# Four weight slots at four other places modulo 512 bytes

## The chip, the cores and the metric

The kernel runs on one core of one Trainium2 chip. The metric is the device time of one execution in microseconds (us), the median over runs.

## The reference

One decoder layer on 256 tokens (`S`) of width 2048 (`D`), all in float32. Token mixing has two branches that read one projection: dilated sliding-window attention with 16 heads, and latent attention with 16 heads and a rotary key. Both are projected to width 2048, gated, summed and projected once more. Channel mixing then looks up experts (PEER): 16,384 single-neuron experts, of which 8 heads choose 16 each per token.

```python
proj = h @ w_in[l]
qa, ka, va, cq, ckv, kr, gate_pre = jnp.split(proj, IN_SPLITS, axis=-1)
...
y_a = y_a @ a_w_out[l]
...
y_b = y_b @ mla_w_out[l]
mix = (g_a * y_a + g_b * y_b) @ w_out[l]
h = layer_norm(ALPHA * h + mix, ln1_g[l], ln1_b[l])
y_p = peer(h, peer_w_query[l], peer_sub_keys_1[l], peer_sub_keys_2[l],
           peer_expert_down[l], peer_expert_up[l])
h = layer_norm(ALPHA * h + y_p, ln2_g[l], ln2_b[l])
...
def chunk(args):          # in peer(): xt tokens, et chosen experts, gt their gates
    xt, et, gt = args
    u = expert_down[et]
    h = jax.nn.gelu(jnp.einsum('cd,ced->ce', xt, u), approximate=False)
    vv = expert_up[et]
    return jnp.einsum('ce,ced->cd', gt * h, vv)
```

## The kernel before

All weights stand in one array, `stream`, in the order in which they are used: 425 tiles of 128 x 2048 float32, each in two halves of 128 x 1024 (4096 bytes per partition). A half goes through a pipeline of four slots, `slot = 2 * (tile % 2) + half`:

- SyncE loads the half into `raw[:, slot, :]`;
- ScalarE copies it to `w_hi[:, slot, :]`, rounded to the type fp32r (L355);
- VectorE writes the rest, `raw - w_hi`, to `w_lo[:, slot, :]` (L611);
- TensorE multiplies with `w_hi` and `w_lo` and then counts the half as used (`half_used`), which frees the slot.

Activations are split in the same way (`a_hi`, `a_lo`; `b_hi`, `b_lo`; `c_hi`, `c_lo`; `m_hi`, `m_lo`). Each product is then three matmuls: high by high, high by low, low by high. The experts aren't gathered: all 128 x 128 of them are computed, and a table `g_dram` of gates, zero where an expert isn't chosen, weighs them.

There are two shapes of product. Up to the down projections (`T_DN`), `three()` (L1011) loads a block of 128 x 128 weights and streams 256 columns of activations; a half is 8 blocks by 3, 24 matmuls. In a block, the operands alternate: `w_hi` with `a_hi`, `w_hi` with `a_lo`, `w_lo` with `a_hi`. In the last stage (`T_UP`, up projections), `up()` (L1208) exchanges the roles: it loads 128 x 128 of `m_hi` or `m_lo` and streams 512 columns of a slot; a half is 24 matmuls too. Weight blocks are 512 bytes apart, blocks of activations 1024 bytes, blocks streamed in the last stage 2048 bytes. So all matmuls of a slot have the same start modulo 512 bytes.

The place of a tensor follows from the order of the `sb(...)` calls, since each goes behind the last. `raw` starts at byte 16,512 of the partition, `w_hi` at 32,896 and `w_lo` at 49,280; each slot of them is 128 modulo 512. Behind them stand `small` (320 bytes), `stat` and `carrier` (64 each), which bring `a_hi`, `a_lo`, `res` and `cst` to 64 modulo 512. `gap_b` (384 bytes) does so for all that follows: `b_hi`, `b_lo`, `c_hi`, `c_lo`, `gate_a`, `head`, `m_hi`, `m_lo`. Nothing uses the gap.

The order on every engine is written out by hand with semaphores. Between the projections, TensorE has short work for attention (transposes L1058, scores L1052, products with `v`), sums by a matmul with `ones` (L1102, L1162; plain float32), and the scores of the keys (L1177).

Of the kernel before, what the change touches and what calls it, by code (L numbers as in the profile page):

```python
# [75 lines left out]
C_ID = C_ROPE + T  # L76
C_ONE = C_ID + P
C_IOTA = C_ONE + P
C_SLOPE = C_IOTA + P
C_TOKEN = C_SLOPE + HEADS  # L80
N_CONST = C_TOKEN + 16

# [46 lines left out]
def build(nc, stream, x_t, const_in, small_in, keys_t, ln2, y_out, a_dram, g_dram):  # L129
    ctx = ExitStack()  # L130

    def sb(name, shape, dt=F32, stack=ctx):
        return stack.enter_context(nc.sbuf_tensor(name, shape, dt))
# [3 lines left out]


    raw = sb("raw", [P, 4, HALF])
    w_hi = sb("w_hi", [P, 4, HALF], F32R)  # L140
    w_lo = sb("w_lo", [P, 4, HALF], F32R)
    small = sb("small", [P, N_SMALL])
    stat = sb("stat", [P, 16])
    carrier = sb("carrier", [P, 16])
    a_hi = sb("a_hi", [P, KD, T], F32R)
    a_lo = sb("a_lo", [P, KD, T], F32R)
    res = sb("res", [P, KD, T])
    cst = sb("cst", [P, N_CONST])
    sb("gap_b", [P, 96])

    mix_mem = ExitStack()
    b_hi = sb("b_hi", [P, KD, T], F32R, mix_mem)
# [99 lines left out]

    ident = col(C_ID, P)
    ones = col(C_ONE, P)
    iota = col(C_IOTA, P)
    block = ctx.enter_context(nc.Block())


# [86 lines left out]
    def _(act):  # L345
# [4 lines left out]
        def hi(t, halves=(0, 1)):  # L350

            for hf in halves:
                act.wait_ge(raw_in[t.slot(hf)], t.pair * 16 + 16)
                act.wait_ge(half_used, t.half(hf) + 1)
                act.activation(w_hi[:, t.slot(hf), :], raw[:, t.slot(hf), :], ACT.Copy).then_inc(hi_ready, 1)  # L355

        def done(t):
            act.wait_ge(half_used, t.half(1) + 1 + HALVES_FREE)
# [240 lines left out]
    def _(dve):  # L599
# [6 lines left out]
        def lo(t, halves=(0, 1)):  # L606

            for hf in halves:
                s = t.slot(hf)
                dve.wait_ge(hi_ready, t.half(hf) + 1)  # L610
                dve.tensor_tensor(w_lo[:, s, :], raw[:, s, :], w_hi[:, s, :].bitcast(F32), ALU.subtract).then_inc(lo_ready, 1)  # L611

        def done(t):
            dve.wait_ge(half_used, t.half(1) + 1 + HALVES_FREE)
# [386 lines left out]
    def _(pe):  # L1001
# [4 lines left out]

        def three(out, w_slot, c0, cn, act_h, act_l, first, last):

            wh, wl = w_hi[:, w_slot, c0:c0 + cn], w_lo[:, w_slot, c0:c0 + cn]
            for q, (w, a) in enumerate(((wh, act_h), (wh, act_l), (wl, act_h))):  # L1010
                ins = pe.matmul(out, w, a, start=first and q == 0, stop=last and q == 2)  # L1011
            return ins
# [186 lines left out]
        def up(t, n, b):  # L1199
            pe.wait_ge(mlo_ready, n + 1)  # L1200
            for hf in range(2):
                half_ready(t, hf)
                for tt in range(TT):
                    s = slice(P * tt, P * tt + P)
                    for m, w in ((m_hi, w_hi), (m_hi, w_lo), (m_lo, w_hi)):
                        for c in range(2):
                            o = D * tt + HALF * hf + 512 * c
                            ins = pe.matmul(ps[:, o:o + 512], m[:, b % 2, s], w[:, t.slot(hf), 512 * c:512 * c + 512],  # L1208
                                            start=False, stop=False, skip_group_check=True)
                ins.then_inc(half_used, 1)  # L1210

        def up_bank(t, b, tt, c):

            s = slice(P * tt, P * tt + P)
            o = D * tt + 512 * c
            w = slice(512 * (c % 2), 512 * (c % 2) + 512)
            pe.matmul(ps[:, o:o + 512], m_hi[:, b % 2, s], w_hi[:, t.slot(c // 2), w], start=False, stop=False, skip_group_check=True)
            pe.matmul(ps[:, o:o + 512], m_hi[:, b % 2, s], w_lo[:, t.slot(c // 2), w], start=False, stop=False, skip_group_check=True)
            return pe.matmul(ps[:, o:o + 512], m_lo[:, b % 2, s], w_hi[:, t.slot(c // 2), w], start=False, stop=False,
                             skip_group_check=True)  # L1220

        with pe.Fori(0, NKEYS // 8 - 1) as i:
# [20 lines left out]
def _constants():  # L1243

    c = np.zeros((P, N_CONST), np.float32)
    for b, (qt, kt) in enumerate(((0, 0), (1, 0), (1, 1))):
        q = np.arange(P)[:, None] + P * qt
        k = np.arange(P)[None, :] + P * kt
        d = q - k
        count = np.zeros((P, P), np.float32)  # L1250
        for window, dilation in PATTERNS:
            count += (d >= 0) & (d <= window) & (d % dilation == 0)
        s = slice(P * b, P * b + P)
        c[:, C_D:][:, s] = -d
        c[:, C_NA:][:, s] = np.where(count > 0, 0.0, NEG)
        c[:, C_NB:][:, s] = np.where(d >= 0, 0.0, NEG)
        c[:, C_C:][:, s] = count
    half = ROPE // 2
    inv_freq = np.float32(10000.0) ** (-np.arange(half, dtype=np.float32) / np.float32(half))
    ang = (np.arange(T, dtype=np.float32)[:, None] * inv_freq[None, :]).T  # L1260
    cos, sin = np.cos(ang), np.sin(ang)
    c[:, C_ROPE:C_ROPE + T] = np.concatenate([cos, cos, -sin, sin])
    c[:, C_ID:C_ID + P] = np.eye(P)
    c[:, C_ONE:C_ONE + P] = 1.0
    c[:, C_IOTA:C_IOTA + P] = np.arange(P)
    c[:, C_TOKEN:C_TOKEN + TT] = np.arange(P)[:, None] + P * np.arange(TT)[None, :]
    c[:, C_SLOPE:C_SLOPE + HEADS] = 2.0 ** (-8.0 * np.arange(1, HEADS + 1) / HEADS)
    return c
# [56 lines left out]
```

## Time and profile before

| | |
|---|---|
| median of three runs | 2482.05 us (2477.62 to 2502.12) |
| profiled execution: time, span | 2486.35 us, 2484.7 us |
| mean granted TensorE clock | 0.992 |
| TensorE matmul busy | 2450.2 us, 17,964 matmuls |
| VectorE, ScalarE, GpSimd busy | 1463.2, 1160.5, 549.1 us |
| HBM | 209 GB/s over the span |

Busy time is the union of an engine's instructions. A matmul's record covers its whole way through the array, so those of neighbours overlap; the interval from start to start is what one costs in a dense row. "PEld" is TensorE's weight load, which runs beside the matmul ahead of its own.

### The profile page before, as it was taken

The numbers are of one execution on the slowest core, as the hardware profiler recorded it, in microseconds if no ns is written. First come the engines' busy times: TensorE is split into PE (matmuls) and PEld (weight loads), VectorE is DVE, ScalarE is ACT, GpSimd is POOL, SyncE is SP. The second block draws the span as 40 slices with busy tenths as digits, with TensorE's granted clock in tenths as the row PEclk, the third lists the DMA queues.
The fourth block names the chain that finished last, engine by engine and source line by source line (L and its number), as shares of the span: only waits on it lengthen the run. The fifth ranks groups of instructions, "written<-read, shape, count | busy, mean of one in ns | idle before, by whom it ended". The sixth has DMA issues, their size and how long they took to land.

```text
span 2484.7 us, 49759 instructions
## 1 busy us (share of the span) xinstructions
PE 2450.2 (99%) x17964; PEld 2310.8 (93%) x17964; DVE 1463.2 (59%) x2391; ACT 1160.5 (47%) x1626; POOL 549.1 (22%) x379
## 2 busy tenths in 40 slices
PE   8999999999999998999999999999999999999997
PEld 8999999999999997999999999999888888888886
DVE  5555554546666655378888744444555555555556
ACT  4444444544444434455555544444444444444444
POOL 0000000000000003048888888810000000000000
PEclk9999999999999997999999999999999999999999
DMA  7667666554445653567788888876667666776664
GB/s 265 224 223 225 215 220 200 186 174 152 160 147 183 199 190 123 184 181 209 205 218 216 221 215 216 220 245 221 222 244 243 238 233 235 242 242 242 241 229 145
DMA packets 179840, 521.12 MB, mean 210 GB/s; under 512 B 52768, under 2 KB 52768, under 8 KB 179536
## 3 DMA queue, kind: packets, MB, share of 16 engines
q1 hardware_dynamic: 124128, 449.89, 54.2%
q0 software_dynamic: 51056, 53.89, 9.9%
q10 hardware_dynamic: 4608, 16.78, 1.7%
q8 instruction: 21, 0.34, 0.1%
q14 instruction: 27, 0.22, 0.0%
HBM read 484.70 MB, written 35.78 MB: 209 GB/s over the span
## 4 chain that ended last, share of the span: by engine, by line
PE 97%; DVE 2%; issue 1%; ACT 0%; DMA 0%; DVEq 0%; ACTq 0%
PE ps L1011 65%; PE ps L1208 28%; PE ps L1050 1%; PE ps L1065 1%; PE ps L1058 0%; PE ps L1052 0%; PE ps L1162 0%; PE ps L1177 0%; PE ps L1066 0%; PE ps L1045 0%; DVE a_lo L802 0%; DVE u_s L964 0%; DVE w_lo L611 0%; DVE u_s L974 0%; DVE y_s L951 0%
## 5 line engine op out<-in xcount | busy, mean ns | idle before, releaser
L611 DVE TENSOR_TENSOR w_lo<-raw,w_hi 128x1024 fp32r<-128x1024 f32 x850 | 1015.3, 1223 | 774.8 <-ACT w_hi L355 771.0
L1011 PE MATMUL ps<-a_hi,w_hi 128*128 128x256 f32 x3984 | 1121.0, 281 | 14.6 <-DVE w_lo L611 9.8
L1011 PE MATMUL ps<-a_lo,w_hi 128*128 128x256 f32 x3984 | 1110.0, 279 | 0.0
L1011 PE MATMUL ps<-a_hi,w_lo 128*128 128x256 f32 x3984 | 1109.9, 279 | 0.0
L355 ACT ACTIVATE w_hi<-raw 128x1024 fp32r<-128x1024 f32 x850 | 866.8, 1054 | 255.5 <-PE ps L1208 179.4
L1011 PEld LDWEIGHTS ps<-a_hi,w_hi 128*128 128x128 f32 x3984 | 752.9, 189 | 19.6 <-issue 15.3
L1011 PEld LDWEIGHTS ps<-a_lo,w_hi 128*128 128x128 f32 x3984 | 755.8, 190 | 0.5
L1011 PEld LDWEIGHTS ps<-a_hi,w_lo 128*128 128x128 f32 x3984 | 754.1, 189 | 0.0
L326 POOL DMA_INDIRECT g_dram<-gate_v,where x256 | 462.1, 1805 | 195.2 <-DVE gate_v L882 117.5
L1208 PE MATMUL ps<-w_lo,m_hi 128*128 128x512 f32 x1008 | 314.3, 393 | 0.0
L1208 PE MATMUL ps<-w_hi,m_hi 128*128 128x512 f32 x1008 | 312.7, 391 | 0.0
L1208 PE MATMUL ps<-w_hi,m_lo 128*128 128x512 f32 x1008 | 311.5, 390 | 0.0
L1208 PEld LDWEIGHTS ps<-w_hi,m_lo 128*128 128x128 f32 x1008 | 189.3, 188 | 43.1
L1208 PEld LDWEIGHTS ps<-w_lo,m_hi 128*128 128x128 f32 x1008 | 189.6, 188 | 40.9
L1208 PEld LDWEIGHTS ps<-w_hi,m_hi 128*128 128x128 f32 x1008 | 189.5, 188 | 39.9
L541 ACT ACTIVATE act<-ps 128x256 f32<-128x256 f32 x128 | 49.1, 384 | 323.6 <-PE ps L1011 322.4
L316 POOL DMA_DIRECT2D a_in<-a_dram x32 | 17.0, 532 | 751.7 <-DVE m_f L918 749.6
L535 ACT ACTIVATE m_hi<-m_f 128x256 fp32r<-128x256 f32 x128 | 53.4, 417 | 208.8 <-DVE m_f L918 208.8
L1011 PE MATMUL ps<-b_hi,w_hi 128*128 128x256 f32 x512 | 142.9, 279 | 0.0
L1011 PE MATMUL ps<-b_lo,w_hi 128*128 128x256 f32 x512 | 141.6, 277 | 0.0
L1011 PE MATMUL ps<-b_hi,w_lo 128*128 128x256 f32 x512 | 141.6, 276 | 0.0
L308 POOL TENSOR_SCALAR res<-res,small 128x256 f32<-128x256 f32 x16 | 18.0, 1139 | 503.1 <-DVE a_lo L802 503.1
(172 smaller groups left out, 1710.9 us busy)
## 6 DMA issues: line engine op xcount, KB each, us to landing
raw<-stream SPq DMA_DIRECT2D x850, 512.0 KB, 4.2
g_dram<-blank POOLq DMA_DIRECT2D x32, 512.0 KB, 6.2
a_dram<-act ACTq DMA_DIRECT2D x32, 512.0 KB, 3.6
a_in<-a_dram POOLq DMA_DIRECT2D x32, 512.0 KB, 4.9
g_in<-g_dram POOLq DMA_DIRECT2D x32, 512.0 KB, 6.2
g_dram<-gate_v,where POOLq DMA_INDIRECT x256
res<-x_t SPq DMA_DIRECT2D x4, 512.0 KB, 6.9
ln_s<-ln POOLq DMA_DIRECT2D x1, 2048.0 KB, 11.6
```

The source lines that it names most:

```text
L308: ins = pool.tensor_scalar(res[:, k, :], res[:, k, :], small[:, S_B1 + k:S_B1 + k + 1], None, ALU.add)
L316: pool.dma_start(a_in[:, b], a_dram[i * 2 + b]).then_inc(ag_in[b], 16)
L326: pool.indirect_dma_start(out=g_cell, out_offset=bass.IndirectOffsetOnAxis(ap=where[:, tt, k:k + 1], axis=0), in_=gate_v[:, tt, k:k + 1], ...
L355: act.activation(w_hi[:, t.slot(hf), :], raw[:, t.slot(hf), :], ACT.Copy).then_inc(hi_ready, 1)
L535: act.activation(m_hi[:, par, :], m_f[:, par, :], ACT.Copy).then_inc(mhi_ready, 1)
L541: act.activation(act4[:, b // 4, b % 4, :], acc[t.par][:, 0:T], ACT.Gelu).then_inc(acc_free[t.par], 1)
L611: dve.tensor_tensor(w_lo[:, s, :], raw[:, s, :], w_hi[:, s, :].bitcast(F32), ALU.subtract).then_inc(lo_ready, 1)
L1011: ins = pe.matmul(out, w, a, start=first and q == 0, stop=last and q == 2)
L1050: ins = pe.matmul(ps_s[:, o:o + k1], q_s[:, q0:q0 + P], k_s[:, 0:k1], start=True, stop=not rope)
L1065: pe.matmul(ps_o[:, 0:T], v_s[:, 0, :], p_t[:, 0:T], start=True, stop=False, skip_group_check=True)
L1208: ins = pe.matmul(ps[:, o:o + 512], m[:, b % 2, s], w[:, t.slot(hf), 512 * c:512 * c + 512], start=False, stop=False, skip_group_check=True)
```

## The change

`w_hi` and `w_lo` become four tensors each, one for each slot, and unused gaps and the small tensors `stat` and `carrier` stand between them, so that each slot has a start of its own modulo 512 bytes, the same for its high and its low part. To make room, `small` moves behind `cst` and takes the place of `gap_b` with it (320 bytes), and the constant `iota` shrinks from 128 to 16 columns, of which 16 were read.

| slot | start before, modulo 512 | start after (`w_hi`, `w_lo`) | after, modulo 512 |
|---|---|---|---|
| 0 | 128 | 32,928 and 53,920 | 160 |
| 1 | 128 | 37,120 and 58,112 | 256 |
| 2 | 128 | 41,280 and 62,272 | 320 |
| 3 | 128 | 45,504 and 49,600 | 448 |
| activations | 64 | `a_hi` 66,624, `b_hi` 124,480 | 64 |

`raw` stays where it was, and so does everything from `b_hi` on. `a_hi`, `a_lo`, `res` and `cst` move by 512 bytes or a few more and remain at 64 modulo 512. Each engine has the same instructions in the same order as before.

```diff
-C_SLOPE = C_IOTA + P
+C_SLOPE = C_IOTA + TOPK
...
     raw = sb("raw", [P, 4, HALF])
-    w_hi = sb("w_hi", [P, 4, HALF], F32R)
-    w_lo = sb("w_lo", [P, 4, HALF], F32R)
-    small = sb("small", [P, N_SMALL])
+    sb("gap0", [P, 8])
+    w_hi0 = sb("w_hi0", [P, HALF], F32R)
+    sb("gap1", [P, 24])
+    w_hi1 = sb("w_hi1", [P, HALF], F32R)
     stat = sb("stat", [P, 16])
+    w_hi2 = sb("w_hi2", [P, HALF], F32R)
+    sb("gap3", [P, 32])
+    w_hi3 = sb("w_hi3", [P, HALF], F32R)
+    w_lo3 = sb("w_lo3", [P, HALF], F32R)
     carrier = sb("carrier", [P, 16])
+    sb("gap4", [P, 40])
+    w_lo0 = sb("w_lo0", [P, HALF], F32R)
+    sb("gap5", [P, 24])
+    w_lo1 = sb("w_lo1", [P, HALF], F32R)
+    sb("gap6", [P, 16])
+    w_lo2 = sb("w_lo2", [P, HALF], F32R)
+    sb("gap7", [P, 64])
+    w_hi, w_lo = (w_hi0, w_hi1, w_hi2, w_hi3), (w_lo0, w_lo1, w_lo2, w_lo3)
     a_hi = sb("a_hi", [P, KD, T], F32R)
     a_lo = sb("a_lo", [P, KD, T], F32R)
     res = sb("res", [P, KD, T])
     cst = sb("cst", [P, N_CONST])
-    sb("gap_b", [P, 96])
+    small = sb("small", [P, N_SMALL])
...
-    iota = col(C_IOTA, P)
+    iota = col(C_IOTA, TOPK)
...
-            wh, wl = w_hi[:, w_slot, c0:c0 + cn], w_lo[:, w_slot, c0:c0 + cn]
+            wh, wl = w_hi[w_slot][:, c0:c0 + cn], w_lo[w_slot][:, c0:c0 + cn]
...
-    c[:, C_IOTA:C_IOTA + P] = np.arange(P)
+    c[:, C_IOTA:C_IOTA + TOPK] = np.arange(TOPK)
```

The other lines of the diff write `w_hi[s][:, ...]` where `w_hi[:, s, ...]` stood.

## Rows read from the trace of the kernel before

**Rows 1.** The page: busy time by engine, and the chain that ended last

```profile
PE 2450.2 (99%) x17964; PEld 2310.8 (93%) x17964; DVE 1463.2 (59%) x2391; ACT 1160.5 (47%) x1626; POOL 549.1 (22%) x379
...
PE ps L1011 65%; PE ps L1208 28%; PE ps L1050 1%; PE ps L1065 1%; PE ps L1058 0%; PE ps L1052 0%; PE ps L1162 0%; PE ps L1177 0%; PE ps L1066 0%; PE ps L1045 0%; DVE a_lo L802 0%; DVE u_s L964 0%; DVE w_lo L611 0%; DVE u_s L974 0%; DVE y_s L951 0%
```

**Rows 2.** The waits of TensorE's matmuls: us in total, times, longest us

```profile
PE ps L1011 <- DVE w_lo L611: 9.8, 2, 9.1
PE ps L1011 <- DVE a_lo L802: 4.5, 1, 4.5
```

**Rows 3.** L1011 by operands: duration min/median/max in ns, first and last start

```profile
L1011 PE MATMUL ps<-a_hi,w_hi x3984: 275/276/583, 9.1 to 1764.1; 128*128 128x256 f32 x200
...
L1011 PE MATMUL ps<-b_hi,w_hi x512: 275/276/370, 540.8 to 928.1; 128*128 128x256 f32 x171
...
L1011 PE MATMUL ps<-c_hi,w_hi x256: 280/281/469, 535.2 to 744.1; 128*128 128x256 f32 x128
```

**Rows 4.** Groups by line: count | busy us, mean ns of one | idle before

```profile
L611 DVE TENSOR_TENSOR w_lo<-raw,w_hi 128x1024 fp32r<-128x1024 f32 x850 | 1015.3, 1223 | 774.8 <-ACT w_hi L355 771.0
L355 ACT ACTIVATE w_hi<-raw 128x1024 fp32r<-128x1024 f32 x850 | 866.8, 1054 | 255.5 <-PE ps L1208 179.4 <-PE ps L1011 47.7 <-ACT act L541 24.3
...
L1208 PE MATMUL ps<-w_lo,m_hi 128*128 128x512 f32 x1008 | 314.3, 393 | 0.0
```

**Rows 5.** Windows: busy PE, PEld, DVE, ACT, POOL (count); clock, DMA, GB/s

```profile
421.00:534.00 113.00, 113.00 (x956) 112.79 (x954) 56.94 (x57) 56.23 (x80) 0.31 (x1) 1.00 0.55 181
1061.00:1247.00 186.00, 186.00 (x1582) 186.00 (x1581) 147.21 (x433) 104.42 (x135) 138.29 (x79) 1.00 0.76 204
1300.00:1740.00 440.00, 440.00 (x3885) 440.00 (x3884) 239.76 (x410) 205.05 (x267) 281.45 (x156) 1.00 0.78 222
1800.00:2440.00 640.00, 640.00 (x2797) 525.52 (x2797) 374.28 (x466) 284.25 (x349) 37.41 (x58) 1.00 0.69 238
```

**Rows 6.** TensorE in order of time, about 1247.1 us: start us, us

```profile
1246.98 0.28 PE L1011 MATMUL ps<-a_lo,w_hi 128*128 128x256 f32 x1
1247.10 0.28 PE L1011 MATMUL ps<-a_hi,w_lo 128*128 128x256 f32 x1
1247.49 0.38 PE L1011 MATMUL ps<-a_hi,w_hi 128*128 128x256 f32 x1
...
1248.06 0.28 PE L1011 MATMUL ps<-a_lo,w_hi 128*128 128x256 f32 x1
1248.17 0.28 PE L1011 MATMUL ps<-a_hi,w_lo 128*128 128x256 f32 x1
```

**Rows 7.** The same about 418.6 us, and L1102's durations as in rows 3

```profile
418.65 1.89 PE L1102 MATMUL ps<-head,cst 128*128 128x256 f32 x8
...
420.73 0.28 PE L1011 MATMUL ps<-a_hi,w_hi 128*128 128x256 f32 x1
420.85 0.28 PE L1011 MATMUL ps<-a_lo,w_hi 128*128 128x256 f32 x1
...
L1102 PE MATMUL ps<-head,cst x16: 377/379/381, 418.7 to 444.5; 128*128 128x256 f32 x16
```

**Rows 8.** The same about 950.5 us, and PE's window (its clock is 0.50)

```profile
950.45 0.41 PE L1011 MATMUL ps<-a_lo,w_hi 128*128 128x256 f32 x1
950.66 0.41 PE L1011 MATMUL ps<-a_hi,w_lo 128*128 128x256 f32 x1
...
949.00:955.00 6.00, 5.99 (x20) 0.50 0.00 0
```

**Rows 9.** TensorE in order of time, behind the three transposes

```profile
63.78 0.49 PE L1058 MATMUL ps<-cst,logit 128*128 128x128 f32 x3
...
64.23 0.28 PE L1011 MATMUL ps<-a_lo,w_hi 128*128 128x256 f32 x1
...
64.82 0.28 PE L1011 MATMUL ps<-a_hi,w_hi 128*128 128x256 f32 x1
64.93 0.28 PE L1011 MATMUL ps<-a_lo,w_hi 128*128 128x256 f32 x1
```

More of the change, by code:

```diff
@@ L354, in hi @@
                 act.wait_ge(half_used, t.half(hf) + 1)
-                act.activation(w_hi[:, t.slot(hf), :], raw[:, t.slot(hf), :], ACT.Copy).then_inc(hi_ready, 1)
+                act.activation(w_hi[t.slot(hf)][:, :], raw[:, t.slot(hf), :], ACT.Copy).then_inc(hi_ready, 1)
         def done(t):
@@ L610, in lo @@
                 dve.wait_ge(hi_ready, t.half(hf) + 1)
-                dve.tensor_tensor(w_lo[:, s, :], raw[:, s, :], w_hi[:, s, :].bitcast(F32), ALU.subtract).then_inc(lo_ready, 1)
+                dve.tensor_tensor(w_lo[s][:, :], raw[:, s, :], w_hi[s][:, :].bitcast(F32), ALU.subtract).then_inc(lo_ready, 1)
         def done(t):
@@ L1207, in up @@
                             o = D * tt + HALF * hf + 512 * c
-                            ins = pe.matmul(ps[:, o:o + 512], m[:, b % 2, s], w[:, t.slot(hf), 512 * c:512 * c + 512],
+                            ins = pe.matmul(ps[:, o:o + 512], m[:, b % 2, s], w[t.slot(hf)][:, 512 * c:512 * c + 512],
                                             start=False, stop=False, skip_group_check=True)
@@ L1216, in up_bank @@
             w = slice(512 * (c % 2), 512 * (c % 2) + 512)
-            pe.matmul(ps[:, o:o + 512], m_hi[:, b % 2, s], w_hi[:, t.slot(c // 2), w], start=False, stop=False, skip_group_check=True)
-            pe.matmul(ps[:, o:o + 512], m_hi[:, b % 2, s], w_lo[:, t.slot(c // 2), w], start=False, stop=False, skip_group_check=True)
-            return pe.matmul(ps[:, o:o + 512], m_lo[:, b % 2, s], w_hi[:, t.slot(c // 2), w], start=False, stop=False,
+            pe.matmul(ps[:, o:o + 512], m_hi[:, b % 2, s], w_hi[t.slot(c // 2)][:, w], start=False, stop=False, skip_group_check=True)
+            pe.matmul(ps[:, o:o + 512], m_hi[:, b % 2, s], w_lo[t.slot(c // 2)][:, w], start=False, stop=False, skip_group_check=True)
+            return pe.matmul(ps[:, o:o + 512], m_lo[:, b % 2, s], w_hi[t.slot(c // 2)][:, w], start=False, stop=False,
                              skip_group_check=True)
```

## The prediction

> **What bounds the kernel now.** The totals by engine come first: TensorE is busy for 2450.2 of 2484.7 us, and the chain of work that ended last runs through it for 97%, 65% at the line of the 256-column products and 28% at that of the 512-column products [rows 1]. Next come TensorE's own waits. They add up to some 20 us, the largest 9.8 us, most of it at the start [rows 2]. So the time is the number of matmuls times the interval from the start of one to the start of the next. Busy time doesn't give that interval, since the records of matmuls overlap (each lasts 0.28 us); windows do, because they count how many fall in a stretch.
>
> The counts: 3 x (3984 + 512 + 256) = 14,256 products of 256 columns and 3 x 1008 = 3,024 of 512 columns [rows 3, 4]. The intervals, with a window's count less the one or two matmuls that had begun before it: 440 us / 3883 = 113.3 ns from 1300 to 1740 us, 186 / 1580 = 117.7 ns from 1061 to 1247 us, and 640 / 2795 = 229.0 ns in the last stage [rows 5]. The first two are the same code with the same operands (the down projections, `a_hi` and `a_lo` against the slots) at the same granted clock of 1.00, and differ by 4.4 ns. The change from the one to the other lies at 1247.10 us, where one half tile came 0.39 us after the matmul ahead of it: within five matmuls the interval is 0.11 instead of 0.12 us, and it stays there (the window above begins 52 us later) [rows 6]. The opposite change is at 418 to 421 us, behind eight matmuls with `ones` [rows 7]. So an interval isn't a constant of the shape. It has at least two stable values, and the way in which TensorE comes out of an interruption decides between them. A moving stream and the weight load for the next matmul run side by side in every interval; that they disturb each other by an amount that depends on how they lie is my reading of this, and the trace doesn't show it directly.
>
> The floor is seen twice. While the granted clock is at its lower level (1.2 GHz), the same products follow each other within 0.21 us, 950.45 to 950.66 [rows 8], so the columns alone take half of it at 2.4 GHz, 106.7 ns. And the eight matmuls with `ones` start from 418.65 to 420.16 us (their end at 420.54 less 0.379), 215.7 ns each [rows 7]; that is 2.3 ns over twice 106.7 ns. Against that the 256-column products now pay 6.6 or 11.0 ns over the columns, and the 512-column ones 229.0 - 213.4 = 15.6 ns.
>
> How the time splits: 948 matmuls at 421 to 534 us (956 less the eight with `ones`), 1582 at 1061 to 1247 us, and the 768 with `c_hi` and `c_lo`, whose least duration of 280 ns is 5 ns over that of the `b_hi` ones in the same loop, are at the slower value [rows 3, 5]. That is 3,298 of them; some 10,960 are at the faster one.
>
> **The change part by part.** No instruction is added, removed or moved on any engine. What moves is where the weight slots start: in bytes modulo 512, 128 for all before, and 160, 256, 320, 448 after. Activations stay at 64. The distance from the moving stream's start to that of the weights being loaded is 64 for all now; it becomes 96, 192, 256 and 384. In the last stage the roles are exchanged (the slot streams, `m_hi` and `m_lo` are loaded), and the distance goes from -64 to -96, -192, -256 and -384. The trace of before has weight products at one distance alone, so what another distance costs has no row; it is bounded by the values that the intervals take at this one.
>
> - The 256-column products. Best: all excess over the columns goes, 10,960 x 6.6 + 3,298 x 11.0 = 72 + 36 = 108 us. A less extreme end keeps 2.3 ns each: 108 - 33 = 75 us. Worst that a row shows: all that are at 113.3 go to 117.7, 10,960 x 4.4 = +48 us. I take half of the latter, **+24 us**: two slots of four at the slower value. The reason for a loss and not a gain is the nearest row: 77% of these products sit at the lower of two values at the present distance, and the only other value that the trace has of this shape at this clock lasts longer. That a new distance has a value under 113.3 has no row at all.
> - The seams. Now every slot has the same distance, so a stable interval lasts through hundreds of matmuls. Afterwards the distance is another one every 24 matmuls, and the streams may have to settle again. What settling costs is seen behind the three transposes at 63.78 us: the five intervals from 64.23 to 64.82 us take 0.59 us, and then they are 0.11 us each [rows 9]. That is some 20 ns over five of the faster kind (0.567 us). 14,256 / 24 = 594 half tiles by 20 ns is **+12 us**. The bounds are 0, and twice it.
> - The 512-column products. Best: 3,024 x 15.6 = 47 us less, or 40 us with 2.3 ns kept. Worst: one more step of 4.4 ns, +13 us. Their excess is the largest, and a distance of -64 may be a bad one for them or not; I take **0**, with both ends in the range.
> - ScalarE and VectorE. They write and read the slots at the new places: 1.05 and 1.22 us a half tile [rows 4]. In the fullest stretch VectorE is busy for 147.21 of 186 us [rows 5], with 1582 / 24 = 66 of its 433 instructions the `w_lo` ones; 10% on those is 8 us, inside the 39 us that it has free. The cover is thin at one place: the half tile at 1247.44 us was late by some 0.3 us [rows 6], and there the cost would be another 0.1 us a time. **0**, at most +2.
> - `small`, `stat`, `carrier` and the constants. `stat` and `small` feed short instructions of ScalarE and VectorE, which are off the path, and the constants lose 112 of 2208 columns of one load of which only the first 16 were read. **0**.
>
> The sum against the profiled execution: 2486.35 + 24 + 12 = 2522 us. That execution is 4.3 us over the median of the runs, 2482.05, so the forecast for the median is **2518 us, +1.4%**.
>
> **A rule that speaks against any effect.** The matmuls at 1100 and at 1400 us differ by 4.4 ns with the same operands [rows 5], so something besides the column count is in the interval. The Trainium skill, page "TensorE: Matmul & The Clock Gate", section "Step-by-step: what each phase is for", says that TensorE has "two independent SBUF read ports" and that loading the next weights takes no read bandwidth from the running matmul. By that rule no place of a slot can matter, and the median would stay at 2482 us. The trace doesn't refute it, since its one distance can't, but it says nothing on the two values. The same page, section "Back-to-back issue gap", gives columns / 2.4 + 2.5 ns, that is 109.2 and 215.8 ns; the trace is 4 to 13 ns above that in every weight product, and has the sum only for the matmuls with `ones`.
>
> **The rivals.**
>
> *The place doesn't matter.* What sets 113.3, 117.7 and 229.0 ns is the rate of the moving stream and how the two streams are set off, not where they lie. For it: the operands `a` and `b` have the same least duration [rows 3], and coming out of an interruption alone changes it [rows 6, 7]. Against it: it leaves open what the streams meet in. Time: 2482, within 10 us either way (ends of interruptions fall differently, 948 matmuls by 4.4 ns are 4 us).
>
> *Faster.* The streams meet in the same part of memory, the present 64 bytes are near enough for the load to be always just ahead of the stream, and more distance takes them apart. It decides from where a slot's interval falls under 113.3 ns. For it: the excess is 15.6 ns where the stream is twice as long, and gone for the matmuls with `ones`, which read at half the rate. Price, at half the way to the floor: the faster kind 2.2 ns less (24 us), the slower kind down to the same 111 ns (22 us), a third of the excess over 215.6 ns in the last stage (4.5 x 3,024 = 14 us): 60 us, so 2422 us. With one good slot of four it is a quarter of that, 2467 us, inside the case above.
>
> *Slower, but by more than I forecast.* All four slots at 117.7 ns, settling at 12 us, the last stage one step up: 48 + 12 + 13 = 73 us, 2555 us.
>
> **How the numbers follow.** A difference under 1% (25 us) is about what a measurement of this kernel can't tell from none. Slower by the forecast's mechanism, with its larger form: 0.44. No effect of the place, or gains and losses of slots that cancel: 0.30. Faster: 0.26. The likeliest case alone spans 2507 to 2555 us. The range goes from 2430 us (it leaves out about half of the faster case) to 2560 us (it leaves out what lies over the worst form, some 0.05).
>
> **What would show each step.** In windows of 10 us or less, the four slots, told apart by their order in a tile and in the next, should have different intervals: two near 113 and two near 118 ns. If all are 113.3 and the switch at 1247 us is still there, the place doesn't matter. Right behind each half tile's first matmul I expect four or five intervals of 117 to 121 ns; if they are missing, the 12 us go. The last stage should stay at 229 ns on average, with values that differ by slot. ScalarE's and VectorE's means should stay at 1054 and 1223 ns. I am wrong if any slot lies under 112 ns or the last stage under 226: then the present place was a bad one, not a good one. I am wrong in size if an interval over 120 ns appears, for which the trace has no row.

## The result: 1.8% slower

The changed kernel takes 2534.76 us in the median of four runs (2533.67 to 2535.89), against 2490.86 us of before, measured beside it (2477.62 to 2502.12). The ratio is 1.0178, 95% interval [1.0116, 1.024]. The four runs of before fall into two pairs, 2477.62 and 2482.05 us and 2499.66 and 2502.12 us, and their median lies between them; against the 35 runs of the kernel before that the later experiments had beside them, median 2485.86 us, the ratio would be 1.020. The forecast was 2518 us, with a range of 2430 to 2560. The profiled execution took 2534.17 us with a span of 2532.5 us, 47.8 us over the span of before.

First one slip in the words ahead of the prediction: in the last stage a half tile has 12 matmuls, not 24; 24 are a tile. A half of the last stage is then 12 matmuls wherever it is counted below, and no number of the prediction uses the slip.

**Where the time isn't.** The page of the changed kernel, the chain of work that ended last:

```profile
PE 97%; DVE 2%; issue 1%; ACT 0%; DMA 0%; DVEq 0%; ACTq 0%; SPq 0%
PE ps L1024 66%; PE ps L1221 28%; PE ps L1063 1%; PE ps L1078 1%; PE ps L1071 0%; PE ps L1065 0%; PE ps L1175 0%; PE ps L1190 0%; PE ps L1079 0%; PE ps L1058 0%; DVE a_lo L815 0%; DVE u_s L977 0%; DMA raw<-stream 0%; DVE w_lo L624 0%; DVE u_s L987 0%
```

And its waits of TensorE's matmuls, and the groups of the two engines that fill the slots:

```profile
PE ps L1024 <- DVE w_lo L624: 10.3, 3, 9.0
PE ps L1024 <- DVE a_lo L815: 4.5, 1, 4.5
...
L624 DVE TENSOR_TENSOR w_lo<-raw,w_hi 128x1024 fp32r<-128x1024 f32 x850 | 1015.3, 1224 | 816.0 <-ACT w_hi L368 812.9
L368 ACT ACTIVATE w_hi<-raw 128x1024 fp32r<-128x1024 f32 x850 | 867.2, 1054 | 267.0 <-PE ps L1221 188.1 <-PE ps L1024 50.4 <-ACT act L554 24.3
```

The lines answer to [rows 1, 2, 4]. TensorE's two largest waits are 0.5 us more, and ScalarE and VectorE take 1054 and 1224 ns for a half tile, as before to a nanosecond. They only wait longer: VectorE for ScalarE (812.9 us against 771.0), and ScalarE for TensorE to free the slots (188.1 and 50.4 us against 179.4 and 47.7). So what is left for the 48 us is the intervals of TensorE's matmuls; the sum below is the check.

**Where it is.** The windows of the changed kernel over the stretches of [rows 5]:

```profile
421.00:534.00 113.00, 113.00 (x953) 112.58 (x953) 57.68 (x57) 57.21 (x79) 0.31 (x1) 1.00 0.56 177
1061.00:1247.00 186.00, 185.42 (x1586) 185.22 (x1586) 137.30 (x400) 104.09 (x141) 119.95 (x69) 1.00 0.72 194
1300.00:1740.00 440.00, 440.00 (x3755) 440.00 (x3755) 241.66 (x450) 201.11 (x262) 296.76 (x166) 1.00 0.78 215
```

From 1300 to 1740 us there are 3755 matmuls instead of 3885: 440 / 3753 = 117.2 ns, against 113.3 ns. From 1061 to 1247 us, where the kernel before was at its slower value (1582), there are about as many as before (1586). The DMA engines and the granted clock show no cause: the clock is 1.00 in all these rows, and less is moved per second, not more.

The intervals of single slots are seen in the list in order of time. These are the first matmuls of five half tiles, slots 0, 1, 2, 3 and 0 again, each 24 matmuls behind the one ahead:

```profile
1505.10 0.28 PE L1024 MATMUL ps<-a_hi,w_hi 128*128 128x256 f32 x1
...
1507.92 0.28 PE L1024 MATMUL ps<-a_hi,w_hi 128*128 128x256 f32 x1
...
1510.64 0.28 PE L1024 MATMUL ps<-a_hi,w_hi 128*128 128x256 f32 x1
...
1513.52 0.28 PE L1024 MATMUL ps<-a_hi,w_hi 128*128 128x256 f32 x1
...
1513.86 0.29 PE L1024 MATMUL ps<-a_hi,w_hi 128*128 128x256 f32 x1
1513.99 0.28 PE L1024 MATMUL ps<-a_lo,w_hi 128*128 128x256 f32 x1
...
1516.36 0.28 PE L1024 MATMUL ps<-a_hi,w_hi 128*128 128x256 f32 x1
```

They are 2.82, 2.72, 2.88 and 2.84 us long, by 24: 117.5, 113.3, 120.0 and 118.3 ns. The same count over all half tiles from 1300 to 1740 us gives 117.22 ns (slot 0, start 160), 113.33 (slot 1, 256), 119.96 (slot 2, 320) and 118.37 (slot 3, 448), and half tiles of one slot differ by under 0.1 ns. Their mean is 117.2. Inside a half tile of the slots 0 and 3 the single intervals are uneven. One of slot 3 is 0.13 us (1513.86 to 1513.99), and by the trace's starts in ns they run from 113 to 124 ns over this half tile, in a pattern that comes again. The interval of such a slot is thus a mean over 24 matmuls; in slot 1 all are 113 or 114 ns. One slot of four is as fast as before, and one is slower than anything that the trace of before shows.

In the last stage the same is done with 12 matmuls for each half. Here the list merges matmuls in pairs; slots 0, 1, 2, 3, 0 begin at

```profile
2000.39 0.63 PE L1221 MATMUL ps<-w_hi,m_hi 128*128 128x512 f32 x2
...
2003.19 0.62 PE L1221 MATMUL ps<-w_hi,m_hi 128*128 128x512 f32 x2
...
2005.98 0.62 PE L1221 MATMUL ps<-w_hi,m_hi 128*128 128x512 f32 x2
...
2008.72 0.62 PE L1221 MATMUL ps<-w_hi,m_hi 128*128 128x512 f32 x2
...
2011.51 0.39 PE L1221 MATMUL ps<-w_hi,m_hi 128*128 128x512 f32 x1
```

2.80, 2.79, 2.74 and 2.79 us by 12 are 233.3, 232.5, 228.3 and 232.5 ns; over the whole stage 233.27, 232.98, 228.33 and 232.64, a mean of 231.8. Before it was 228.9 ns in all slots. The counts of the same window, first the kernel before and then the changed one:

```profile
1850.00:2440.00 590.00, 590.00 (x2579) 1.00 0.70 239
1850.00:2440.00 590.00, 590.00 (x2547) 1.00 0.71 235
```

The sum: 3,024 x 2.9 = +9 us for the last stage. For the rest the mean before was (10,958 x 113.33 + 3,298 x 117.78) / 14,256 = 114.4 ns, and 14,256 x (117.2 - 114.4) = +40 us. Together 49, measured 47.8. The split can be read directly: the last stage's first 512-column matmul starts at 1805.5 us instead of 1766.7, 38.8 us later, and from it to the last one at L1221 (L1208 before) it is 700.9 us instead of 692.1, 8.8 us more.

### The profile page after: what moved, and what is told of

Same layout as the page of the kernel before. It is cut to its first block, busy times and chain, and to the rows that moved or that the text cites. A ratio compares the mean times of both kernels' runs of the same rounds, so it can differ in the third digit from the quotient of the medians.

```text
span 2532.5 us, 49758 instructions
## 1 busy us (share of the span) xinstructions
PE 2497.4 (99%) x17963; PEld 2348.3 (93%) x17964; DVE 1461.9 (58%) x2391; ACT 1162.6 (46%) x1626; POOL 546.2 (22%) x379
## 4 chain that ended last, share of the span: by engine, by line
PE 97%; DVE 2%; issue 1%; ACT 0%; DMA 0%; DVEq 0%; ACTq 0%; SPq 0%
PE ps L1024 66%; PE ps L1221 28%; PE ps L1063 1%; PE ps L1078 1%; PE ps L1071 0%; PE ps L1065 0%; PE ps L1175 0%; PE ps L1190 0%; PE ps L1079 0%; PE ps L1058 0%; DVE a_lo L815 0%; DVE u_s L977 0%; DMA raw<-stream 0%; DVE w_lo L624 0%; DVE u_s L987 0%
## 5 line engine op out<-in xcount | busy, mean ns | idle before, releaser
L624 DVE TENSOR_TENSOR w_lo<-raw,w_hi 128x1024 fp32r<-128x1024 f32 x850 | 1015.3, 1224 | 816.0 <-ACT w_hi L368 812.9
L368 ACT ACTIVATE w_hi<-raw 128x1024 fp32r<-128x1024 f32 x850 | 867.2, 1054 | 267.0 <-PE ps L1221 188.1
L1221 PE MATMUL ps<-w_lo,m_hi 128*128 128x512 f32 x1008 | 315.9, 394 | 0.0
L1221 PE MATMUL ps<-w_hi,m_hi 128*128 128x512 f32 x1008 | 315.1, 393 | 0.0
L1221 PE MATMUL ps<-w_hi,m_lo 128*128 128x512 f32 x1008 | 314.9, 393 | 0.0
L1221 PEld LDWEIGHTS ps<-w_hi,m_lo 128*128 128x128 f32 x1008 | 189.0, 188 | 45.3
L1221 PEld LDWEIGHTS ps<-w_hi,m_hi 128*128 128x128 f32 x1008 | 189.0, 188 | 44.4
L1221 PEld LDWEIGHTS ps<-w_lo,m_hi 128*128 128x128 f32 x1008 | 189.0, 188 | 44.2
```

The lines of the kernel that those rows point to most:

```text
L368: act.activation(w_hi[t.slot(hf)][:, :], raw[:, t.slot(hf), :], ACT.Copy).then_inc(hi_ready, 1)
L624: dve.tensor_tensor(w_lo[s][:, :], raw[:, s, :], w_hi[s][:, :].bitcast(F32), ALU.subtract).then_inc(lo_ready, 1)
L1221: ins = pe.matmul(ps[:, o:o + 512], m[:, b % 2, s], w[t.slot(hf)][:, 512 * c:512 * c + 512], start=False, stop=False, skip_group_check=True)
```

## The experiments

Three theories were put to the test. **D**: the interval of a slot is set by the distance, modulo some power of two, from the start of the moving stream to the start of the weights that are loaded beside it. **P**: the place of the slot itself counts, whatever the activations' is. **M**: what costs is that neighbouring slots have different places. "Interval" below is always start of a half tile to start of the next, by the number of its matmuls, mean over the stretch from 1300 to 1740 us for 256 columns, and from 1850 to 2440 us for 512. The diffs are excerpts; the comments in them give the start modulo 512 bytes and aren't in the kernels.

### Everything moved by 64 bytes, distance kept

```diff
     raw = sb("raw", [P, 4, HALF])
+    sb("gap_s", [P, 16])
     w_hi = sb("w_hi", [P, 4, HALF], F32R)
```

(an edit of the kernel before; all the other excerpts but that of "m alone" are edits of the changed kernel)

> The kernel before with everything behind raw moved up by 64 bytes: slots at 192, activations at 128 modulo 512, so the distance from the moving stream to the weights being loaded stays 64. Theory D (the interval is set by the distance of the two streams modulo 512): as before, 113.3 or 117.8 ns for 256 columns, 228.9 ns for 512 columns, about 2486 us. Theory P (the absolute place of a slot decides): other intervals than these, 2 to 7 ns away, so 2500 us or more. Theory M (what costs is that neighbouring slots differ): as before as well.

Measured: 2481.27 us, one run, 2487.0 us for the kernel before beside it. The intervals are those of before: 113.33 or 117.78 ns and 228.89 ns. Its windows (TensorE alone: us, busy, clock, DMA share, GB/s):

```profile
421.00:534.00 113.00, 113.00 (x955) 1.00 0.56 180
1061.00:1230.00 169.00, 169.00 (x1494) 1.00 0.78 210
1300.00:1740.00 440.00, 440.00 (x3885) 1.00 0.79 222
1850.00:2440.00 590.00, 590.00 (x2580) 1.00 0.71 237
```

P falls: 128 and 192 are the same place when the activations move along, and the slot start of 192, with the activations left at 64, has 118.8 ns in the second map below. One thing is new. From 1061 to 1230 us this kernel is at 169 / 1492 = 113.3 ns, where the kernel before has 117.7, and the query projections ahead of it (975 to 1045 us) are at 117.78 where that one has 113.33. So the two values are no property of a stage. They are chosen anew at an interruption. The run also moves the slots against `raw`, which stays, and the intervals don't change.

### Three maps

Four slots at four places each, the gaps between the tensors changed for it (`stat` and `carrier` fill some); here the first, in short:

```diff
+    stat = sb("stat", [P, 16])
+    carrier = sb("carrier", [P, 16])
+    sb("gap0", [P, 64])
     w_hi0 = sb("w_hi0", [P, HALF], F32R)      # 0 modulo 512
+    sb("gap1", [P, 8])
     w_hi1 = sb("w_hi1", [P, HALF], F32R)      # 32
...
```

> Four slots at 0, 32, 64, 96 modulo 512, activations at 64: distances -64, -32, 0, 32 in the 256-column products. Theory D: each slot has an interval of its own that settles within a few matmuls, and it differs from slot to slot by some ns; the slot at distance 0 isn't known; mean between 113 and 120 ns, 2480 to 2560 us. Theory M: all four near 117 ns as in the changed kernel, whatever the distance.

> Four slots at 192, 224, 288, 352: distances 128, 160, 224, 288. The neighbours measured so far are 96 (117.2 ns), 192 (113.3), 256 (120.0), 384 (118.4). Theory D: values between 113 and 120 ns that differ by slot; 2500 to 2560 us. Theory M: all near 117 ns.

> Four slots at 128, 384, 416, 480: distances 64, 320, 352, 416. Theory D: the slot at 128 shows 113.3 or 117.8 ns as in the kernel before, though its neighbours lie elsewhere, and 228.9 ns in the last stage; the others between 113 and 120 ns. Theory M: the slot at 128 shows some 117 ns and 232 ns in the last stage, like the mean of the changed kernel.

Measured, one run each: 2547.88, 2552.86 and 2532.19 us. All that the runs so far give, by start of the slot:

| slot start | run | 256 columns: distance | ns | last stage: distance | ns |
|---|---|---|---|---|---|
| 0 | first map | 448 | 117.78 | 64 | 233.1 |
| 32 | first map | 480 | 117.95 | 32 | 233.0 |
| 64 | first map | 0 | 119.8 | 0 | 228.7 |
| 96 | first map | 32 | 118.2 | 480 | 233.6 |
| 128 | before, all slots | 64 | 113.33 (117.78) | 448 | 228.9 |
| 128 | third map | 64 | 113.4 | 448 | 233.2 |
| 160 | changed kernel | 96 | 117.2 | 416 | 233.3 |
| 192 | second map | 128 | 118.8 | 384 | 232.5 |
| 224 | second map | 160 | 119.8 | 352 | 234.0 |
| 256 | changed kernel | 192 | 113.33 | 320 | 233.0 |
| 288 | second map | 224 | 116.8 | 288 | 233.4 |
| 320 | changed kernel | 256 | 119.96 | 256 | 228.3 |
| 352 | second map | 288 | 118.2 | 224 | 233.4 |
| 384 | third map | 320 | 113.5 | 192 | 233.3 |
| 416 | third map | 352 | 120.1 | 160 | 234.1 |
| 448 | changed kernel | 384 | 118.4 | 128 | 232.6 |
| 480 | third map | 416 | 119.4 | 96 | 233.8 |

In the 256-column stages the slots differ by up to 7 ns, against M, and the slot at 128 keeps its 113.4 ns with other neighbours. All four distances that are 64 modulo 128 (64, 192, 320, 448) have 113.3 or 117.8 ns, the pair of values of the kernel before; those at 0 modulo 128 and the ones between lie from 116.8 to 120.1. But the bad ones don't repeat after 128 bytes: the distances of 96, 224, 352 and 480 have 117.2, 116.8, 120.1 and 117.95 ns. Whether that is a longer period or the neighbours is open, for of the bad distances only 256 was run with all slots at it. So a period of 128 bytes is seen for the good distances alone. In the last stage only distances 0 and 256 are near 228.5 ns. But the slot at 128 has 233.2 ns there among other slots and 228.9 among its like, at the same distance. So in the last stage the slots ahead count as well, as M says, and a row of this table holds only for its neighbours.

### All slots at the slowest place

```diff
     raw = sb("raw", [P, 4, HALF])
-    sb("gap0", [P, 8])
+    stat = sb("stat", [P, 16])
+    carrier = sb("carrier", [P, 16])
+    sb("gap0", [P, 16])
     w_hi0 = sb("w_hi0", [P, HALF], F32R)      # 320
-    sb("gap1", [P, 24])
     w_hi1 = sb("w_hi1", [P, HALF], F32R)      # 320, and so on to w_lo3
...
```

> All four slots at 320 modulo 512 (distance 256 to the activations, the slowest slot of the changed kernel at 120.0 ns), activations and m at 64. Theory D (distance): 120.0 ns in all slots of all 256-column stages, 5.6 ns over the kernel before on average by 14,256 matmuls, that is +80 us; the last stage near 228.5 ns as that slot had it; some 2565 us. Theory M (mixed neighbours cost): nothing is mixed, so 113.3 or 117.8 ns and 229 ns, 2480 to 2500 us.

Measured: 2554.7 us in one run, 2484.37 us for the kernel before beside it. In the windows:

```profile
421.00:534.00 113.00, 113.00 (x932) 1.00 0.55 173
1061.00:1230.00 169.00, 168.42 (x1411) 1.00 0.68 187
1300.00:1740.00 440.00, 440.00 (x3669) 1.00 0.78 210
1850.00:2440.00 590.00, 590.00 (x2604) 1.00 0.72 241
```

440 / 3667 = 120.0 ns, and the interval is 120.00 ns in every slot and, but for the first matmuls behind an interruption, in every stage. Nothing is mixed here, so M falls for the 256-column stages: it is the distance of 256 that costs, 6.7 ns a matmul. The last stage is at 590 / 2602.5 = 226.7 ns, 2.2 ns under the kernel before, and 1.7 ns under the 228.3 of the same slot start when mixed. The total is 10 us below D's 2565, and 7 us of that is the last stage.

### Another good distance, and m moved along

```diff
-    sb("gap0", [P, 8])
+    stat = sb("stat", [P, 16])
+    carrier = sb("carrier", [P, 16])
     w_hi0 = sb("w_hi0", [P, HALF], F32R)      # 256, and so on to w_lo3
...
+    sb("gap_m", [P, 32], F32, up_mem)
     m_f = sb("m_f", [P, 2, T], F32, up_mem)
```

> All four slots at 256 (distance 192, 113.3 ns in slot 1 of the changed kernel), activations at 64, and m_hi, m_lo at 192, so that in the last stage the distance from the streamed slot to the loaded m is -64 as in the kernel before. Theory D: 113.3 or 117.8 ns and 228.9 ns, as fast as the kernel before, 2475 to 2500 us. If only the distance 64 itself were good, or the place of the slots counted: 117 to 120 ns, over 2530 us.

Measured: 2520.31 us in one run. The windows:

```profile
50.00:400.00 350.00, 350.00 (x3010) 1.00 0.69 220
1300.00:1740.00 440.00, 440.00 (x3738) 1.00 0.78 214
1850.00:2440.00 590.00, 590.00 (x2580) 1.00 0.72 239
```

The last stage is at 228.89 ns, as D says: its distance is -64 like that of before, with both operands elsewhere. The 256-column stages have the pair of values too. From 40 to 400 us six half tiles of eight are at 113.33 ns; but behind 422 us all are at 117.78 ns, also through the whole stretch in which the kernel before is at 113.33. That is some 490 of the 594 half tiles, where the kernel before has about 140. So my number of at most 2500 us was missed. The distance of 192 has the same two values as 64, and which of them is taken is a matter of its own, worth up to 14,256 x 4.4 = 63 us.

### One slot at another good distance

```diff
     w_hi3 = sb("w_hi3", [P, HALF], F32R)      # 128, as w_hi0 and w_hi2 ahead
+    stat = sb("stat", [P, 16])
+    carrier = sb("carrier", [P, 16])
+    w_hi1 = sb("w_hi1", [P, HALF], F32R)      # 256
+    w_lo1 = sb("w_lo1", [P, HALF], F32R)      # 256
+    sb("gap0", [P, 96])
     w_lo0 = sb("w_lo0", [P, HALF], F32R)      # 128, as w_lo2 and w_lo3 behind
```

> Slot 1 alone at 256, the other three at 128 as before. Theory D: all four slots at 113.3 or 117.8 ns in the 256-column stages; in the last stage slots 0, 2, 3 at 228.9 ns and slot 1 at 233.0 ns as in the changed kernel, +3 us; 2480 to 2495 us. Theory M: slots 1 and 2, behind a seam, above the others in both kinds of stage; the slot at 128 in the third map run had 233.2 ns in the last stage, which speaks for M there: 233 ns in all four, +12 us.

Measured: 2481.31 us in one run (before beside it: 2484.37). Slots 0, 2 and 3 are at 228.9, 229.2 and 228.9 ns in the last stage and slot 1 at 232.4, near D's numbers and not M's 233 in all four. From 1300 to 1740 us all four slots are at 113.33 ns, the two at a seam too, against M again. The surprise is in the stages that lie at 117.8 ns in the kernel before:

```profile
421.00:534.00 113.00, 113.00 (x985) 1.00 0.60 188
1061.00:1230.00 169.00, 169.00 (x1494) 1.00 0.82 217
```

There are 985 matmuls from 421 to 534 us against 956. The half tiles that begin at 419.6, 422.6, 425.5 and 428.3 us (slots 2, 3, 0, 1) are still at 117.78 ns, and the next one, behind slot 1, is at 113.33, with no interruption between them. Behind the second group of `ones` the same comes again: the four half tiles from 443.5 us (slots 2, 3, 0, 1) are at 117.78 and those from 455.0 us on at 113.33. It isn't so everywhere: from 557 to 740 us the half tiles at 117.78 are the same as in the kernel before. In the next stretch (169 / 1492 = 113.3 ns) this kernel is at the faster value from the start.

### The low parts alone

```diff
     w_hi3 = sb("w_hi3", [P, HALF], F32R)      # 128, as w_hi0 to w_hi2
+    stat = sb("stat", [P, 16])
+    carrier = sb("carrier", [P, 16])
+    sb("gap0", [P, 16])
     w_lo0 = sb("w_lo0", [P, HALF], F32R)      # 320, as w_lo1 to w_lo3
```

> The high parts of all slots at 128 as before, the low parts at 320. Of three weight loads in the 256-column stages one is then at distance 256. Theory D, each load priced alone: the mean of three intervals is (2 x 113.3 + 120.0) / 3 = 115.6 ns, +17 us on the stages at 113.3 ns, 2500 us. If any disturbed load sets the pace of all three: 118 to 120 ns, 2540 us or more.

Measured: 2540.1 us in one run.

```profile
1061.00:1230.00 169.00, 168.42 (x1436) 1.00 0.72 192
1300.00:1740.00 440.00, 440.00 (x3739) 1.00 0.79 213
1850.00:2440.00 590.00, 590.00 (x2548) 1.00 0.70 237
```

All 256-column stages are at 117.78 ns, but for half tiles behind an interruption, and not at 115.6. Pricing each load alone is wrong: it would give 115.6 ns, or (2 x 117.8 + 120.0) / 3 = 118.5 ns from the slower value. But that one bad load in three costs 4.4 ns isn't shown either. 117.78 ns is also the slower value of the good distances, and the run ahead, with no load at a bad distance, has it in the same stretch, with the same count to one matmul (3738 and 3739). The run shows that the faster value is gone from all stages, not that a new price has come. The last stage is at 231.67 ns. It streams `w_hi` at distance -64 and `w_lo` at -256, which had 228.89 and 226.67 ns each by itself: the mixture within a slot is slower than either (the 590 us hold 2548 matmuls). D has no price for that.

### m alone

```diff
+    sb("gap_m", [P, 80], F32, up_mem)
     m_f = sb("m_f", [P, 2, T], F32, up_mem)
```

(slots and activations as in the kernel before; `m_hi` and `m_lo` come to 384 modulo 512)

> All slots at 128 and activations at 64 as in the kernel before; only m_hi and m_lo move, to 384 modulo 512, so that in the last stage the distance from the streamed slot to the loaded m is 256 (226.67 ns in the run with all slots at 320) and not -64 (228.9). Theory D: 226.67 ns in the last stage, 2.2 ns by 3,024 = 7 us less; 256-column stages as before, with their two values; ratio 0.997. Theory P: no change, or another value in the last stage.

Measured in 12 runs: 2478.48 us (2474.11 to 2499.16), before 2485.86 us in 35 runs (2481.20 to 2506.39); ratio 0.9962 [0.993, 0.9995]. The last stage is at 226.67 ns:

```profile
1850.00:2440.00 590.00, 590.00 (x2605) 1.00 0.72 240
```

All else is as before. The distance of that stage is shown to be worth 7 us by itself, as D says.

### One slot elsewhere, and m

> As the run with slot 1 alone at 256, and m at 384. There the stages that lay at 117.8 ns in the kernel before lay at 113.3 but for one. If the one different slot ends the slower state, that is 3,298 less 768 matmuls by 4.4 ns = 11 us; the last stage has three slots near 226.7 and slot 1 (distance 128) near 232.5 ns, 228.1 on average, 2 us less. Together -13 us, ratio 0.995, and a smaller spread between runs than the kernel before has. If the faster state there was chance: ratio 0.999, and the same spread as before.

> Slot 1 alone at 384 (distance 320, 113.3 or 117.8 ns in the map), m at 384, so that in the last stage slots 0, 2, 3 have distance 256 and slot 1 has 0. Theory D: 113.3 ns in nearly all 256-column stages if the one different slot ends the slower state (-11 us); the last stage at 226.7 in three slots and 227 to 229 ns in slot 1 (-5 us); together -16 us, ratio 0.993. If mixing costs in the last stage, slot 1 and the slot behind it lie over 229 ns and the gain is 10 us or less.

The edits are those of the two runs ahead, with slot 1 at 256 in the one and at 384 in the other.

| kernel | median, us | lowest to highest, runs | ratio to before |
|---|---|---|---|
| slot 1 at 256, m at 384 | 2474.32 | 2473.29 to 2477.04, 12 | 0.9940 [0.9914, 0.9966] |
| slot 1 at 384, m at 384 | 2478.50 | 2475.09 to 2501.28, 12 | 0.9971 [0.9942, 1.0001] |

The windows of the first, and behind it those of the second:

```profile
421.00:534.00 113.00, 113.00 (x985) 1.00 0.57 187
1061.00:1230.00 169.00, 169.00 (x1494) 1.00 0.81 218
1850.00:2440.00 590.00, 590.00 (x2584) 1.00 0.72 237
```

```profile
421.00:534.00 113.00, 113.00 (x955) 1.00 0.56 181
1061.00:1230.00 169.00, 169.00 (x1438) 1.00 0.78 208
1850.00:2440.00 590.00, 590.00 (x2605) 1.00 0.71 240
```

With a slot at distance 192 among slots at 64 the two stretches are fast again (985 and 1494 matmuls); with one at distance 320 they aren't (955 and 1438). In the last stage it is the other way round: distances 256 and 0 mix without loss (226.67 ns in all four slots), while 256 and 128 don't (226.67, 232.64, 227.92, 226.67). So the 11 us hoped for from the second kernel didn't come, and its last stage was better than expected. The first kernel has the lowest median of the study, by what it wins in the two stretches, and its runs lie within 3.8 us of each other.

That spread is a result too. Seven of the 35 runs of the kernel before lie at 2498.8 to 2506.4 us, the others at 2481 to 2490. The down projections behind the interruption at 1247 us are some 4,550 matmuls at 113.3 ns, (1764 - 1248) us / 113.3 ns; if they fall to the slower value, that is 4,550 x 4.4 = 20 us. Two and two of 12 runs of the kernels without a slot at 256 (m alone, slot 1 at 384) have the same 20 us, and none of the 12 and 10 runs of the two kernels measured so often that mix 64 with 192 (the one above and the next). No such run was profiled, so that this is the cause of the 20 us is argued from the size and the pattern, not shown.

### Four places again, all of them good

```diff
-    sb("gap0", [P, 8])
     w_hi0 = sb("w_hi0", [P, HALF], F32R)      # 128 instead of 160
-    sb("gap1", [P, 24])
-    w_hi1 = sb("w_hi1", [P, HALF], F32R)
     stat = sb("stat", [P, 16])
+    carrier = sb("carrier", [P, 16])
+    w_hi1 = sb("w_hi1", [P, HALF], F32R)      # 256; then w_hi2 at 384 instead of 320, w_hi3 at 0 instead of 448
...
```

> Four slots at four places again, but 128, 256, 384 and 0, so that all distances in the 256-column stages (64, 192, 320, 448) are 64 modulo 128; m at 64. Theory D with a period of 128 bytes: 113.3 or 117.8 ns in every slot, so 2475 to 2500 us but for the last stage, where mixed slots had 232 to 233 ns (+9 to +13 us); ratio 1.000 to 1.006. Theory M (four different places cost in themselves): 117 ns on average as in the changed kernel, ratio 1.018.

Measured in 10 runs: 2483.09 us (2481.81 to 2484.56); ratio 0.9978 [0.9953, 1.0003].

```profile
421.00:534.00 113.00, 113.00 (x988) 1.00 0.58 189
1061.00:1230.00 169.00, 169.00 (x1492) 1.00 0.81 215
1300.00:1740.00 440.00, 440.00 (x3885) 1.00 0.79 222
1850.00:2440.00 590.00, 590.00 (x2557) 1.00 0.70 236
```

This is the changed kernel with three slot starts different, and all of its loss is gone: 3885 matmuls against 3755. Four places don't cost in the 256-column stages; four places that aren't 64 modulo 128 from the activations do. In the last stage the slots have 229.23, 232.43, 229.23 and 232.43 ns (distances 448, 320, 192, 64), which fits a period of 256 bytes there, and 2 ns on average are still lost. Here too the slower value ends soon behind an interruption: it lasts two half tiles at 420.3, 444.0 and 1057.7 us. From 557 to 758 us, though, all half tiles have it, twice as many as in the kernel before.

## Why the prediction was right, and where it was off

- **What bounds the kernel.** Right: number of matmuls times interval, and the whole difference is in the intervals.
- **That the two streams disturb each other by how they lie.** It was my reading, and the runs bear it out: the interval changes when one operand is moved against the other (the slots in the 256-column stages, the slots or `m` alone in the last one) and stays when both are moved by the same. Moving the activations alone in the 256-column stages wasn't run. Where in the chip the two reads meet, no run shows. Writes by ScalarE and VectorE into the slots are a poor rival for the 256-column stages: from 1300 to 1740 us the two are busy for 241.66 and 201.11 of 440 us, and yet half tiles of one slot of the changed kernel differ by under 0.1 ns there. By the Trainium skill, page "TensorE: Matmul & The Clock Gate", section "Step-by-step: what each phase is for", the weight load takes no read bandwidth from the running matmul. Taken as a rule for the time, that doesn't hold here: it is 6.7 ns of 113.3 between two places of the same tensors. The prediction also held the trace against columns / 2.4 + 2.5 ns. In the section "Back-to-back issue gap" of the same page of the Trainium skill that is the gap of a matmul by itself, while the spacing in a row of loads and matmuls is set by both. So the 4 to 13 ns above it were no contradiction, and nothing in the sum used them.
- **The 256-column products, +24 us.** Right in sign and mis-sized: they cost some 40 us. The reason for the sign was not sound: I took the second value at the old distance as a sample of what a new distance does, and the runs show that the two values are there at each good distance. That the sign came out right is in part luck. I took two slots at 113.3 and two at 117.7 ns; they are at 117.2, 113.3, 120.0 and 118.4. The upper bound of +48 us held for the sum, not for the slots: it was taken from the slower of two values at one distance, and another distance has higher ones (120.0 ns).
- **The seams, +12 us.** Wrong. The intervals of a slot settle at once: the half tiles of slot 1 take 24 x 113.3 ns with the seam in them. The settling that I read behind the transposes belongs to coming out of an interruption, and I carried it to a place that has none. The 12 us stood in the sum for part of what the two other terms lacked (24 + 12 + 0 = 36 against 40 + 0 + 9 = 49), so the total came nearer than its terms.
- **The 512-column products, 0.** Mis-sized, and put at nothing with a reason for neither side: it is +9 us, within the +13 us of its upper end. That these stages could also gain was right as a bound: at distance 256 they do, 2.2 ns.
- **ScalarE, VectorE, constants, 0.** Right.
- **The rivals.** "The place doesn't matter" is refuted by the slots' intervals. "Faster", by more distance taking the streams apart, is refuted as a mechanism: distances of 96, 128, 160 and 256 have 117.2 to 120.0 ns, and no slot of any run has a mean under 113.3. With good places at 64, 192, 320 and 448 and bad ones between, it can't be a matter of more or less distance. "Slower, but by more", 2555 us, had all slots at 117.7 ns and the seams; the 2534.76 us lie about halfway between it and the forecast, but one slot stayed at 113.3 and the seams cost nothing.
- **The two values, 113.3 and 117.8 ns.** I treated them as how far a new place could go. They are both there at each good distance, independent of the question of the change; in the changed kernel slot 1 is at 113.3 ns also from 1061 to 1247 us, where the kernel before has 117.8 in all slots; the mean of the four is near 117.3 there, and the two kernels are equally fast.

What stays open: why a distance of 64 modulo 128 is good in the one stage and 0 modulo 256 in the other, what decides between the two values behind an interruption, why slots at 64 and 192 together end the slower one in some stretches, and whether the bad distances have a period. No run looked at steps finer than 32 bytes.

## What to carry to other kernels

Where TensorE is busy all the time, divide a window's length by its count of matmuls and compare that with the column time; a few ns over it may be an address matter, and are worth a try. Move the streamed and the loaded tensor against each other in steps of 32 bytes, with another place for each buffer of a rotation, so that one profile prices several places; then set all buffers to the good one, since mixed layouts have prices of their own. Here the first place was a good one already: the best layout won 0.6% over it, while bad ones lost up to 2.8%. And look for two values of the same interval in one trace before taking one of them as the cost.

## What the runs showed of the hardware

- A matmul of 256 fp32r columns with a weight load beside it took 113.33, 117.78 or 120.00 ns in kernels with all slots at one place, by the distance of the two operands (64 or 192 bytes against 256) and by the history; in mixed layouts distances of 64, 192, 320 and 448 had 113.3 or 117.8 ns and the twelve others measured 116.8 to 120.1; one of 512 columns 226.67 ns at a distance of 256 and 228.89 at -64, and 226.7 to 234.1 in mixed layouts.
- The same code on the same addresses has two lasting intervals, 113.33 and 117.78 ns. An interruption can change the one to the other in either direction; among slots at distance 64, one at distance 192 ended the slower one after four half tiles, 96 matmuls, behind two interruptions of two kernels; one at 320 didn't end it.
- The interval isn't the mean of what each load would cost: two loads of three at 64 and one at 256 gave 117.78 ns, all three at 256 gave 120.00, and 115.6 or 118.5 would be the mean.
